# Two work buffers of a transformer kernel change places in on-chip memory

## Time and profile before

| | |
|---|---|
| median of 3 runs | 2800.68 us (2800.26 to 2804.02) |
| the profiled execution | 2804.02 us, span in the trace 2802.2 us |
| TensorE busy | 2689.9 us, 96% of the span, 12282 matmuls |
| VectorE busy | 2057.7 us, 73% |
| ScalarE busy | 1626.4 us, 58% |
| GpSimd busy | 243.4 us, 9% |
| TensorE granted clock, mean | 0.981 |
| HBM | 706.57 MB read, 261 GB/s with the writes over the span |

### The profile page before, as it was taken

How to read it: one execution, slowest core, us unless ns; L and a number is a source line. 1 busy time by engine, 2 the same in 40 slices (tenths; PEclk the granted TensorE clock), 3 DMA queues, 4 the chain that set the end, 5 groups by cost and what they waited for, 6 DMA issues and landing times.

```text
span 2802.2 us, 38484 instructions
## 1 busy us (share of the span) xinstructions
PE 2689.9 (96%) x12282; PEld 2157.9 (77%) x12282; DVE 2057.7 (73%) x2438; ACT 1626.4 (58%) x2055; POOL 243.4 (9%) x213
## 2 busy tenths in 40 slices
PE   8996999999999999999999999889999899989999
PEld 5754888888888888888878877777788787867787
DVE  4655999999999999999965567765555545877554
ACT  2322888888888888888844434534344344345443
POOL 0002111111111111111100000000000000200000
PEclk9997999999999999999999999999999999999999
DMA  8745999999999999999956654254466456534554
GB/s 319 252 148 192 354 361 362 360 359 356 369 360 363 361 356 363 363 355 359 361 195 193 192 178 153 98 172 149 146 192 223 129 188 206 157 118 136 168 187 147
DMA packets 263482, 700.34 MB, mean 250 GB/s; under 512 B 29512, under 2 KB 128240, under 8 KB 213680
## 3 DMA queue, kind: packets, MB, share of 16 engines
q1 hardware_dynamic: 249780, 685.19, 69.2%
q0 software_dynamic: 9504, 8.42, 0.9%
q10 hardware_dynamic: 4124, 5.77, 0.6%
HBM read 706.57 MB, written 23.63 MB: 261 GB/s over the span
## 4 chain that ended last, share of the span: by engine, by line
PE 84%; DVE 7%; issue 3%; DMA 3%; ACT 2%; SPq 1%; POOL 1%; POOLq 0%; DVEq 0%; ACTq 0%
PE bank L664 22%; PE bank L666 22%; PE bank L665 22%; PE bank L1173 3%; PE bank L1175 3%; PE bank L1174 3%; PE bank L790 1%; PE bank L814 1%; DMA raw<-in_w_in 1%; PE bank L1046 1%; PE bank L1012 1%; PE bank L1072 1%; PE bank L838 1%; PE bank L738 1%; DVE w_lo L1317 1%
## 5 line engine op out<-in xcount | busy, mean ns | idle before, releaser
L664 PE MATMUL bank<-w_hi,HTh 128*128 128x512 f32 x2824 | 1124.4, 398 | 17.6 <-DVE HTl L1368 9.5
L666 PE MATMUL bank<-w_hi,HTl 128*128 128x512 f32 x2824 | 1102.8, 391 | 0.0
L665 PE MATMUL bank<-w_lo,HTh 128*128 128x512 f32 x2824 | 1102.4, 390 | 0.0
L1317 DVE TENSOR_TENSOR w_lo<-raw,w_hi 128x1024 fp32r<-128x1024 f32 (+3 forms) x406 | 482.2, 1214 | 258.3 <-ACT w_hi L2293 254.0
L2293 ACT ACTIVATE w_hi<-raw 128x1024 fp32r<-128x1024 f32 (+3 forms) x406 | 421.3, 1055 | 418.9 <-PE bank L666 267.1
L664 PEld LDWEIGHTS bank<-w_hi,HTh 128*128 128x128 f32 x2824 | 532.9, 189 | 139.0 <-DVE HTl L1368 13.9
L666 PEld LDWEIGHTS bank<-w_hi,HTl 128*128 128x128 f32 x2824 | 532.6, 189 | 114.5
L665 PEld LDWEIGHTS bank<-w_lo,HTh 128*128 128x128 f32 x2824 | 533.4, 189 | 103.0
L1964 DVE TENSOR_TENSOR w_lo<-arena,w_hi 128x1024 fp32r<-128x1024 f32 x256 | 316.1, 1235 | 38.6 <-ACT w_hi L2491 22.3
L1964 DVE TENSOR_TENSOR w_lo<-raw,w_hi 128x1024 fp32r<-128x1024 f32 x256 | 298.9, 1220 | 3.6 <-ACT w_hi L2536 3.6
L2491 ACT ACTIVATE w_hi<-raw 128x1024 fp32r<-128x1024 f32 x252 | 268.0, 1063 | 55.6 <-PE bank L666 55.6
(11 more groups left out here) (365 smaller groups left out, 2707.9 us busy)
## 6 DMA issues: line engine op xcount, KB each, us to landing
raw<-in_moe_w SPq DMA_DIRECT2D x128, 1024.0 KB, 6.8
arena<-in_moe_w SPq DMA_DIRECT2D x128, 1024.0 KB, 6.6
H<-in_moe_w SPq DMA_DIRECT2D x64, 1024.0 KB
MIX<-in_moe_w SPq DMA_DIRECT2D x64, 1024.0 KB
raw<-in_ffn_w SPq DMA_DIRECT2D x248, 256.0 KB, 3.4
raw<-in_ffn_w_gu SPq DMA_DIRECT2D x164, 256.0 KB, 3.4
raw<-in_w_in SPq DMA_DIRECT2D x76, 512.0 KB, 4.8
raw<-in_ffn_w_down SPq DMA_DIRECT2D x80, 256.0 KB, 3.3
```

What stands on the lines that cost most here:

```text
L664: pe.matmul(acc, xh, wh, start=start, stop=False)
L665: pe.matmul(acc, xh, wl, start=False, stop=False)
L666: return pe.matmul(acc, xl, wh, start=False, stop=stop)
L1317: dve.tensor_tensor(lo_at(n, c), raw_at(n, c), hi_at(n, c).bitcast(F32), ALU.subtract).then_inc(lo_done, 1)
```

## The change

The two declarations of `w_hi` and `w_lo` are moved up, from behind `H` to right behind `raw`. Nothing else is changed: every engine has the same instructions in the same order with the same waits, 4183 rows on TensorE, 1146 on VectorE, 589 on ScalarE, 50 on GpSimd and 412 on SyncE in the program's listing.

```
         raw = sb("raw", [P, RAW, TILE])
+        w_hi = sb("w_hi", [P, PARTS, TILE], F32R)
+        w_lo = sb("w_lo", [P, PARTS, TILE], F32R)
         with ExitStack() as shared:
             arena_r = shared.enter_context(nc.sbuf_tensor("arena_r", [P, 10888], F32R))
         arena = sb("arena", [P, 10888])
 ...
         EXTRA_RAW += [arena[:, a:a + 2 * TILE] for a in IN_ARENA]
-        w_hi = sb("w_hi", [P, PARTS, TILE], F32R)
-        w_lo = sb("w_lo", [P, PARTS, TILE], F32R)
         BIASR = sb("BIAS", [P, 8, S], F32R)
```

## The result

| | before | after |
|---|---|---|
| median | 2802.2 us (2800.3 to 2804.0, 4 runs) | 2848.6 us (2847.4 to 2854.5, 4 runs) |
| ratio, 95% interval | | 1.0166 (1.0152 to 1.0178) |
| span in the trace | 2802.2 us | 2848.0 us |

The change makes the kernel 46 us slower, 1.7%. The forecast was 2845 us, 44 over the median it started from, with a range of 2822 to 2857.

A forecast was written before the change was run, and what follows sets the result against it. The prediction took TensorE to bound the kernel nearly everywhere. Its terms, 21 - 3 + 17 + 8 = 43 us, with a cross-check of 44, gave +44 us: 2845 us against the median, range 2822 to 2857.

The forecast's parts named there:

- The duration step: Start-to-start distance of TensorE's 512-column matmuls on `w_hi` and `w_lo`: 226.7 to 233.3 ns, as on `arena_r`.
- Experts: 32 rounds of 35.67 us: 135 matmuls each gain 4.9 ns, 0.66 us a round, 21 us, less 3 given back.
- Feed-forwards: Four with 11 steps of 16.82 us: 71 matmuls gain 5.8 ns, 0.41 us a step, 17 us taken.
- The other products: Some 1560 remaining matmuls gain 5.9 ns each, 9 us; 8 us taken, 3 at least and 9 at most.
- What is given back: Slower TensorE waits less: 3 us from the experts' 64 low-part waits, 1.5 us in the first 100 us.
- Rounding and rest: ScalarE and VectorE writing `w_hi` and `w_lo` at the new place: 0 within 5 ns a tile, covered by TensorE.
- The operands that keep their remainders: Buffers that move by 32768 bytes, keeping their remainders: 0; `extra` and `BIAS` lie apart and are equally quick.
- remainder by 64: Reading: moving operands at remainder 32 keep 226.7 ns, `arena_r` at 0 or 16 takes 233.3; the new place has 0.
- region: Reading: `arena_r` between bytes 32896 and 76448 is slow, operands above 105120 quick; the new place says 233.3 ns.
- Rival 2: Faster: position against the stationary operand counts, distance under 226 ns; 2691 us, or 2790 with a tenth of that; 5%.
- Rival 1: No effect of the buffers' place, by the skill's rule: 2801 us; 8%.
- Rival 3: Slower distance mostly hidden: experts bound by VectorE or DMA, only feed-forwards and half the rest pay, 2823 us; 7%.

The follow-up runs named there:

- new_place_rem32: The changed kernel with 32 unused bytes in front of `w_hi` and 32 behind `w_lo`, back at remainder 32 by 64: 2848.7 us, ratio 1.0166.
- old_all_rem0: The kernel before with one gap ahead of `X`, moving all buffers from `X` to `BIAS` by 32 bytes: 2803.5 us, ratio 1.0001.
- old_place_rem0: The kernel before with 32 unused bytes in front of `w_hi` and 32 behind `w_lo`, old region, remainder 0: 2849.3 us, ratio 1.0158.

## Why the prediction was right, and where its reading was not

- *The duration step.* Predicted 226.7 to 233.3 ns on `w_hi` and `w_lo`; measured so. It was read from 120 matmuls of the kernel before, 24 of them in the earlier trace rows, and they decided the case.
- *Experts.* Predicted 0.66 us a round less what is hidden, 36.2 to 36.3 us; measured 36.27 us, 19 us in all for 18. The matmuls alone were to add 0.66 us a round and 0.60 arrived, so some 2 us came back where 3 were taken.
- *Feed-forwards.* Predicted 17.2 us a step; measured 17.23, 18 us in all for 17.
- *The other products.* Predicted 8 us; the rest of the span's growth is 9.
- *What is given back.* Predicted 3 us of waits in the experts and 1.5 in the first 100 us. The waits for the experts' low parts fell from 13.2 us in 64 to 10.3 us in 58. Over the whole, the sum of 48.6 us before hiding became 45.8. Of these 2.8 us about 1 was never there: the distances of the 512-column matmuls on the two buffers, those under 0.26 us, grew by 47.5 us in all. The 4.5 us taken were somewhat too much, and the forecast of +44 is 2 us low mainly by that.
- *Rounding and rest.* Predicted 0; VectorE's busy time grew by 1.7 us and ScalarE's by 1.4, covered by TensorE.
- *The operands that keep their remainders.* Predicted 0. `BIAS` with `SELB` went from 226.7 to 230.2 ns: 128 times that is 0.4 us. So a sum over the moved operands alone leaves out a little that their neighbours pay.
- *The reason.* Here the prediction was right by luck in part. It had two readings, remainder by 64 and region, and both are refuted, the first by `new_place_rem32` and `old_all_rem0`, the second by `old_place_rem0`. What counts is the difference of the two operands by 256. The changed kernel has the same difference for `w_hi` as the slow stretch on `arena_r` had, 224, so the number carried over. Another difference would have had another price: by the table above 233.3 ns at 32 and 192 too, but 228.9 at 64 and 238.0 at 20. The mark that was to tell the two readings apart, `arena_r` still at 233.3 ns in its new region, came out as "the remainder is likelier", and would have misled.
- *Rival 2* named the position against the stationary operand, but only as a way to be faster, and wanted a distance below 226 ns. That the position of the two to each other counts was right. Its mechanism was wrong, two reads that meet when their remainders are equal: d = 0, equal remainders, is the best of the 64 differences tried, and the kernel before already had it.
- *Rival 1*, no effect of the place, by the Trainium skill ("SBUF — State Buffer", section "Who interferes with whom": TensorE never waits for another user). The trace disagrees as to the time: 226.7 to 240 ns by place, with no other engine at work. Nothing here shows TensorE waiting for another engine. The table of the same section lists its reads of the moving operand and of the weights as two independent ports; the pace depends on both addresses all the same, and whether that happens at the ports no run shows.
- *Rival 3*, mostly hidden: refuted, 45.8 of 48.6 us reached the end.

## What to carry to other kernels

When an edit moves buffers, work out each matmul operand pair's addresses, not each buffer's alone: here moving less stationary first byte, modulo 256, with both at multiples of 32, set the pace of 512-column three-pass float32 matmuls, to within the 3 or 4 ns by which one and the same pair can differ, and a declaration moved by a few lines cost 1.7%. Sort the matmuls of the trace by the names of their operands and compare start-to-start distances; a buffer that is used seldom may already show what the busy one would cost in its place. A number that carries over is not yet a cause: three padded versions were enough to refute both readings of the same rows.

## What was not expected of the hardware

- The pace of such matmuls depends on the operands' places with all other engines at rest: 226.7 ns at d = 0, 240.0 at worst, period 256 bytes. In the model, 2803 to 2897 us.
- After an interruption the distances pass through other values before they settle, also at d = 0: behind `arena_r` in the earlier trace rows 230, 236, 228, 233 and 231 ns, behind a feed-forward's transposes in the kernel before ten values between 225 and 236.
- The same pair of addresses settled once at 233.3 and once at 236.7 ns in one execution.
- Plain float32 at 512 columns (429 ns a row at three places) and matmuls at the low clock (0.43 us on `arena_r` and on `extra`) do not show it.
- No place brought the distance below 226.6 ns. The Trainium skill, "TensorE: Matmul & The Clock Gate", section "Back-to-back issue gap", gives 512/2.4 + 2.5, about 216 ns, for an isolated matmul, and about 131 ns for each in a sustained stream of weight loads and matmuls. The stream of this case agrees with neither. What the 11 ns over the first figure are is open, and a weight load of 32 columns instead of 128 did not bring them back.
